# Updating all four quarters of the residual before the first rounding remainder, at nine stage ends of a ten-stage fp32 kernel

## The reference

```python
# first block, twice:
x = x + hybrid_mixer(rms_norm(x, attn_norm[l]), ...)   # stage HYBRID
x = x + conv_ffn(rms_norm(x, ffn_norm[l]), ...)        # stage FFN1
# second block, twice (the mixer is a short convolution, then a gated delta rule):
ff = swiglu(rms_norm_2(h, g[0]), ...)                  # stage FFN2
h = h + 0.5 * rms_norm_2(ff, g[1])
mix = mixer(rms_norm_2(h, g[2]), ...)                  # stage SHORT, then stage DELTA
h = h + rms_norm_2(mix, g[3])
ff = swiglu(rms_norm_2(h, g[4]), ...)                  # stage FFN2
h = h + 0.5 * rms_norm_2(ff, g[5])
```

## Time and profile before

| | |
|---|---|
| median of three runs | 2252.02 us (2250.18 to 2253.71) |
| the profiled execution, its own time | 2247.1 us |
| span of its trace, first to last instruction | 2245.3 us |
| TensorE matmuls busy | 2114.8 us, 94% of the span |
| VectorE busy | 1447.5 us, 64% |
| ScalarE busy | 1114.0 us, 50% |
| mean granted clock of TensorE | 0.968 of full |

### The profile page before, as it was taken

The page is one execution under the profiler, slowest core; times in us unless marked ns, Lnnn a source line. Parts: engine busy times, 40 slices in busy tenths (PEclk is TensorE's granted clock), DMA queues, the critical chain, the costliest instruction groups (busy, mean ns, idle before and its releaser), DMA issues.

```text
span 2245.3 us, 41478 instructions
## 1 busy us (share of the span) xinstructions
PE 2114.8 (94%) x15546; PEld 1969.2 (88%) x15546; DVE 1447.5 (64%) x2478; ACT 1114.0 (50%) x1802; POOL 48.6 (2%) x63
## 2 busy tenths in 40 slices
PE   7998999999998999999999999999997898999998
PEld 7977889999978889989998989989987787978997
DVE  4457677775457677776657666666667877457565
ACT  4454455555443455554445454454446566546443
POOL 1002000000002000000000000000000000000000
PEclk9899999999899999999999999999998998999999
DMA  8422355553222445546554555555554433335552
GB/s 248 150 95 85 121 193 185 195 194 132 89 99 83 146 160 196 194 143 214 181 193 164 174 179 186 179 172 187 183 169 122 127 109 114 112 123 183 187 186 95
DMA packets 118577, 350.80 MB, mean 156 GB/s; under 512 B 23505, under 2 KB 36121, under 8 KB 117953
## 3 DMA queue, kind: packets, MB, share of 16 engines
q1 hardware_dynamic: 115248, 336.27, 45.1%
q0 software_dynamic: 3216, 12.97, 2.1%
HBM read 341.85 MB, written 7.34 MB: 156 GB/s over the span
## 4 chain that ended last, share of the span: by engine, by line
PE 73%; DVE 13%; ACT 6%; issue 4%; DMA 2%; POOL 0%; DVEq 0%; ACTq 0%; SPq 0%; POOLq 0%
PE bank L2074 22%; PE bank L2076 21%; PE bank L2075 21%; DVE wlo L1392 5%; ACT whi L934 3%; PE bank L2500 1%; DMA raw<-panels 1%; PE bank L2223 1%; DVE arena L1582 1%; PE bank L2100 1%; DVE arena L1431 1%; PE bank L2283 1%; DVE x L1442 1%; DMA relay<-arena 0%; DMA arena<-relay 0%
## 5 line engine op out<-in xcount | busy, mean ns | idle before, releaser
L2074 PE MATMUL bank<-xhi,whi 128*128 128x256 f32 x3496 | 1007.2, 288 | 14.4 <-DVE xlo L1778 5.4
L2075 PE MATMUL bank<-xlo,whi 128*128 128x256 f32 x3496 | 993.7, 284 | 0.0
L2076 PE MATMUL bank<-xhi,wlo 128*128 128x256 f32 x3496 | 993.1, 284 | 0.0
L1392 DVE TENSOR_TENSOR wlo<-raw,whi 128x1024 fp32r<-128x1024 f32 x623 | 740.1, 1228 | 194.1 <-ACT whi L934 193.1
L2074 PEld LDWEIGHTS bank<-xhi,whi 128*128 128x128 f32 x3496 | 671.9, 192 | 34.0 <-issue 14.6
L2075 PEld LDWEIGHTS bank<-xlo,whi 128*128 128x128 f32 x3496 | 671.7, 192 | 6.1
L2076 PEld LDWEIGHTS bank<-xhi,wlo 128*128 128x128 f32 x3496 | 670.5, 192 | 0.0
L934 ACT ACTIVATE whi<-raw 128x1024 fp32r<-128x1024 f32 x623 | 623.7, 1046 | 57.4 <-DVE arena L1579 21.7
L2074 PE MATMUL bank<-whi,hhi 128*128 128x512 f32 x688 | 276.0, 401 | 12.6 <-DVE hlo L1533 6.3
L2076 PE MATMUL bank<-whi,hlo 128*128 128x512 f32 x688 | 273.9, 398 | 0.0
L2075 PE MATMUL bank<-wlo,hhi 128*128 128x512 f32 x688 | 273.7, 398 | 0.0
(11 more groups left out here) (361 smaller groups left out, 1784.3 us busy)
## 6 DMA issues: line engine op xcount, KB each, us to landing
raw<-panels SPq DMA_DIRECT2D x623, 512.0 KB, 4.3
arena<-w_in POOLq DMA_DIRECT2D x2, 2048.0 KB, 10.2
arena<-relay SPq DMA_DIRECT2D x8, 512.0 KB, 4.1
arena<-gains_in POOLq DMA_DIRECT2D x6, 512.0 KB, 3.9
relay<-arena POOLq DMA_DIRECT2D x4, 512.0 KB, 6.0
relay<-arena SPq DMA_DIRECT2D x4, 512.0 KB, 5.0
bias_table<-arena POOLq DMA_DIRECT2D x1, 1536.0 KB, 35.1
x<-x_in SPq DMA_DIRECT2D x1, 1024.0 KB, 5.0
```

The costliest lines, as they stand in the source:

```text
L1392: dve.tensor_tensor(wlo[slot][:], raw[slot][:], whi[slot][:].bitcast(F32), ALU.subtract) \
L2074: pe.matmul(dst, w_hi, a_hi, start=start, stop=False, skip_group_check=True)
L2075: pe.matmul(dst, w_hi, a_lo, start=False, stop=False, skip_group_check=True)
L2076: return pe.matmul(dst, w_lo, a_hi, start=False, stop=stop, skip_group_check=True)
```

## The change

VectorE updates all four quarters, and then takes the remainders of tiles 0 to 7. One instruction of VectorE, `prepare_tile(s + 1, 0)`, moves from before the update of quarter 3 to behind it, with its wait for `xhi` of tile 0. No other engine's program is changed, and no instruction is added or removed. The last stage has no following one, and its four updates stood together before.

```diff
-                for q in range(QUARTERS - 1):
+                for q in range(QUARTERS):
                     update(q)
-                more = s + 1 < n_stages
-                if more:
-                    prepare_tile(s + 1, 0)
-                update(QUARTERS - 1)
-                if more:
-                    for k in range(1, KT):
+                if s + 1 < n_stages:
+                    for k in range(KT):
                         prepare_tile(s + 1, k)
                     prepare_rstd(s + 1)
```

## The result

The changed kernel takes 2237.0 us (2233.56 to 2240.93, 6 runs) against 2250.92 us for the one before. The ratio of the two is 0.9947 (0.9932 to 0.9962), 8.6 to 15.3 us or 11.9 us at its centre (the medians themselves are 13.9 us apart). The forecast was a gain of 6.5 us and a range that began at 2241 us: the direction was right, and the gain is nearly twice as large and outside the range. The profiled executions lie 10.6 us apart (spans 2245.3 and 2234.7 us).

A forecast was written before the change was run, and what follows sets the result against it. TensorE bounds it (matmuls busy 94%), standing still at nine stage ends. Terms 2.49 + 1.10 + 0.80 + 0.64 + 0.57 + 0.91 = 6.5 us gave 2245.5 us; own range 2242 to 2249, over all 2241 to 2250.5 us.

The forecast's parts named there:

- The wait that is moved costs nothing: At all stage ends: tile 0's remainder behind the fourth update costs nothing; its first product follows 16 transposes, over 1.5 us later.
- The ends of HYBRID and FFN1, 3.6 us: Four full-clock ends: 0.83 us at three, where a later wait exists, and 1.10 us at FFN1 to FFN2.
- The one term of 1.10 us: End of FFN1 to FFN2: with no later wait, TensorE's start 1.10 us sooner counts in full.
- this race: VectorE's remainders against TensorE's products starting 1.10 us sooner: both reach tile 7 near 319.9, costing at most 0.1 us.
- The post-norm ends, 2.9 us: Five post-norm ends: closed gaps partly halved by low clock, 0.40 + 0.40 + 0.64 + 0.57 + 0.91 us.
- that the rise of the clock stands still while the work moves: Choice at low-clock ends: the clock rises at the same moment; otherwise the low ends keep all, a sum of 7.9 us.
- the terms 0.40, 0.91 and 0.57 us: Forecast gains at the post-norm ends FFN2 to SHORT, FFN2 to DELTA and FFN2 to FFN2, in that order.
- Rival A: Post-norm ends: the closed gap also shortens the low clock, 8.2 us gained, or more if falls are missed; chance 0.10.
- B: Next stages: another wait takes the place and the whole gain is lost, 2250 to 2252 us; chance 0.20 together with D.
- C: Stage ends: remainders become late, about 0.7 us lost at each of nine ends, 6.3 us, 2258 us; chance 0.04.
- D: Shifted stages: the clock falls more often, 1.7 us each, three more leaving 1.4 us gain; chance 0.20 together with B.
- A's first case: The end at 1192.6 gets the shorter low stretch, winning 1.7 us more: sum 8.2 us, 2243.8 us.

The follow-up runs named there:

- the second trace: The changed kernel run once more, unaltered, for a second trace against the kernel before: 2235.72 us, ratio 0.9945 (0.9924 to 0.9965).

## Why the prediction was off, step by step

**The wait that is moved costs nothing.** Right. The remainder of tile 0 starts behind the fourth update at 316.03. That is 0.92 us behind the first transposes, the same distance as before (316.41 against 315.49), and the first product does not wait for it.

**The ends of HYBRID and FFN1, 3.6 us.** Right: 0.92 us at each of the four, 3.7 us in the trace and 4.7 us (1.6 to 7.9) by the run with these ends alone. The one term of 1.10 us was 0.2 us too large. TensorE's products did start 1.1 us sooner, but they then keep VectorE's pace, 0.39 us from tile to tile, where the forecast had 0.36 us:

```profile
998.53 0.32 PE L2070 MATMUL bank<-xhi,whi 128*128 128x256 f32 x1
998.92 0.32 PE L2070 MATMUL bank<-xhi,whi 128*128 128x256 f32 x1
```

The forecast saw this race as tight and put at most 0.1 us on it; it costs 0.2 us.

**The post-norm ends, 2.9 us.** This is the step that failed, and in it the choice "that the rise of the clock stands still while the work moves". The sum kept every low stretch of before at its length and halved what was gained in it. Where the stretch did stay, that gave 0.64 us against 0.70 measured (SHORT to FFN2) and 0.40 us against 0.63 (DELTA to FFN2), so the halving itself is close at one end and 0.23 us short at the other. Where a stretch went, the terms 0.40, 0.91 and 0.57 us measured 1.30, 2.33 and 2.20 us. The run with these ends alone gave 6.3 us in place of 2.9.

With no clock in it, the closed gap is worth 0.92 us at each of nine ends, 8.3 us. It was measured at seven of them: the four of HYBRID and FFN1, and the three post-norm ends that kept the full clock in both orders. The clock's part at the post-norm ends, taken over the 10.39 and 9.47 us of a full-clock end, was 60.0 - 52.0 = 8.0 us before and 52.8 - 47.4 = 5.4 us after (6.5 us in the second trace, 6.4 us in the run with these ends alone). So 1.5 to 2.6 us of clock were won there. With the direct gain that is 9.8 to 10.9 us, inside the measured 8.6 to 15.3 us. The remaining 1 to 2 us of the 11.9 us are not assigned. The second HYBRID stage does not supply them for certain. A low stretch early in it, at 520 us in the kernel before, is in all five traces in which FFN1's ends have the old order, and in none of the six in which they have the new. But the stage's length does not follow. It took 286.4 to 286.5 us in four of the five and 289.6 us in the fifth. With the new order it took 284.9 us in three traces (both of the changed kernel among them), and 286.4, 288.0 and 290.8 us in the other three, which had more low clock later in the stage. So the 1.5 us won there in the traces of the changed kernel are not shown to come from the change.

**Rival A was what happened**, at a chance of 0.10. The measured 11.9 us lies between its two cases, 8.2 us and 13.3 us. Its argument against itself, that the long wait of 3.19 us stays, was right for the first stretch of an end, which mostly stayed; it did not hold for the second one. In the first trace of the changed kernel three stretches fewer stand at the ends, in the two others with the new order there two fewer. Rival A also took the gain ahead of DELTA as hidden by the later wait there. It was not: from the first update of `x` to the end of that wait it took 1702.99 - 1681.15 = 21.84 us before (the earlier trace rows and the stretches above) and 1690.72 - 1671.21 = 19.51 us after, with the wait at 2.23 us both times. The DELTA stage did then give 2.3 us back in this execution. Over all traces that stage took 348 to 354 us, in either order, so what an end wins ahead of DELTA cannot be read from one trace. The rule of the Trainium skill (TensorE: Matmul & The Clock Gate, "Part 4: PE-mode transpose") that transposes do not count as activity for the clock, weighed in the prediction against rival A, is contradicted by the runs: 24 transposes held it at 1.00 through five ends.

**Rivals B, C and D.** The later waits did not grow (0.95 us in FFN1, 1.76 us in HYBRID, 2.23 us in DELTA), so B is out. The products kept the remainders' pace, which took 0.2 us of the 1.1 us by which they start sooner at an end, so C is out as a loss. D, more falls, is seen in one place: the DELTA stage of the first trace, which the second trace (350.8 us) does not repeat. Over the whole span the mean granted clock was 0.969 and 0.970 in the two traces of the changed kernel and 0.968 and 0.966 in the two of the kernel before.

**The other edge of the error** is the range. One or two stretches of 1.7 us either way were allowed for the likeliest case, taken as scatter with no sign. But an idle gap was being taken out at nine places, and at the post-norm ends the runs show that this pushes them one way. The lower end of the whole range, 2241 us, is said to be A's first case, but that case comes to 2243.8 us; the second, 2238.7 us, was left out of the range. The measured 2237.0 us lies below both, though 1.1 us of that is the kernel before, whose median was 2250.92 us in this comparison and 2252.02 us in the forecast.

## What to carry to other kernels

In an in-order engine, an instruction that waits for others should not stand ahead of one for which those others wait; here the order cost 0.92 us at each of nine places. When an idle gap of TensorE is closed near a stretch of low clock, price the clock in the direction of fewer stretches too, at what one costs in the trace: here from 0.7 us, where it lay on the transposes and their waits, to 1.6 us, where it lay on work without a pause. Where TensorE must wait for one to three microseconds, some useless transposes into a free bank can be worth as much as the order of the work: 8.6 us here, on top of the change (2235.72 to 2227.16 us), against 8.3 us that the order gave directly.

## What the runs showed of the hardware

- Transposes keep TensorE's clock at its upper level. With 24 of them (2.78 us) in a wait of 3.19 us, the granted clock was 1.00 at all five ends of the changed kernel. With the wait idle, it was below 1.00 at four of the five in each of its two traces (0.71 to 0.85).
- A gap of 1.18 us between two batches of transposes, with only 0.57 us idle ahead of it, was followed by a fall at two of five ends; with a gap of 0.26 us there was none in five.
- A low stretch of 3.4 us cost 1.54 to 1.58 us where TensorE was at work nearly throughout (11.26 against 9.72 us, 11.04 against 9.46 us). It cost 0.70 us at the last end of the kernel before (11.09 against 10.39 us), where it lay on the transposes: there the first eight took 1.77 us in place of 1.07 us, and the idle gap behind them shrank from 1.18 to 0.56 us.
- A wait of TensorE of 2.27 us (2.22 us the second time) was followed by a low stretch at both ends of HYBRID, and with transposes in it there was none.
